# Small TensorE products dealt one head at a time among the steps of full strips

## The reference, cut to what matters

```python
q = l2norm(q) * (dk ** -0.5)          # per head, over 128 channels
k = l2norm(k)
g = jnp.cumsum(chunk(g), axis=-1)     # per head and chunk, one number per token
k_beta = k * beta[..., None]          # beta: one number per head and token
cq = rmsnorm(c_q, mla_q_norm_g)       # latent rows, 3 x 128 channels
ckv = rmsnorm(c_kv, mla_kv_norm_g)    # 2 x 128 channels
o_a = rmsnorm(o_a, gdn_norm_g) * silu(gate_a)     # per head
```

## Time and profile before

| | |
|---|---|
| median of three executions | 3966.07 us (3965.75 to 3969.32) |
| the profiled execution | 3973.19 us, span 3971.4 us |
| mean granted TensorE clock | 0.978 |
| TensorE busy | 3838.2 us of the span |
| VectorE, ScalarE busy | 2845.7 us, 1585.9 us |

### The profile page before, as it was taken

The page is one execution under the profiler, slowest core; times in us unless marked ns, Lnnn a source line. Parts: engine busy times, 40 slices in busy tenths (PEclk is TensorE's granted clock), DMA queues, the critical chain, the costliest instruction groups (busy, mean ns, idle before and its releaser), DMA issues.

```text
span 3971.4 us, 61257 instructions
## 1 busy us (share of the span) xinstructions
PE 3838.2 (97%) x21282; PEld 3185.6 (80%) x21282; DVE 2845.7 (72%) x5169; ACT 1585.9 (40%) x2439; POOL 88.2 (2%) x101
## 2 busy tenths in 40 slices
PE   8999999899989999999999999999979999999998
PEld 7897789545887888888888888888748888888887
DVE  6442266895788789999887777777463997777776
ACT  5201053231219444444484444444321094444443
POOL 0000000000000000000000000000400000000000
PEclk9899999999999999999999999999979999999999
DMA  5214455475433666666625656666764516666664
GB/s 193 80 45 131 154 182 159 139 239 184 144 113 127 191 197 195 191 190 192 193 77 176 189 188 188 189 190 191 176 237 158 167 58 194 188 188 190 189 187 152
DMA packets 203773, 666.53 MB, mean 168 GB/s; under 512 B 35920, under 2 KB 46176, under 8 KB 202480
## 3 DMA queue, kind: packets, MB, share of 16 engines
q1 hardware_dynamic: 166816, 602.71, 48.2%
q0 software_dynamic: 12496, 52.53, 4.3%
q10 hardware_dynamic: 24320, 9.37, 0.9%
HBM read 637.34 MB, written 26.15 MB: 167 GB/s over the span
## 4 chain that ended last, share of the span: by engine, by line
PE 88%; DVE 9%; ACT 1%; DMA 1%; issue 1%; DVEq 0%; SPq 0%; ACTq 0%; POOLq 0%
PE psum L1083 27%; PE psum L1069 17%; PE psum L1071 9%; PE psum L641 7%; PE psum L720 4%; PE psum L695 4%; PE psum L1160 4%; PE psum L1251 3%; PE psum L1149 2%; DVE arena L2351 1%; PE psum L1049 1%; DVE arena L2352 1%; PE psum L1128 1%; DVE arena L2353 1%; PE psum L1425 1%; PE psum L750 1%
## 5 line engine op out<-in xcount | busy, mean ns | idle before, releaser
L1083 PE MATMUL psum<-rows_split_odd,coef_split 128*128 128x512 f32 x2400 | 590.6, 396 | 3.6 <-DVE rows_split_odd L2495 3.6
L1083 PE MATMUL psum<-rows_split,coef_split 128*128 128x512 f32 x2208 | 532.1, 390 | 0.3 <-issue 0.3
L2500 DVE TENSOR_REDUCE work<-psum 128x256 f32<-128x512 f32 x360 | 249.1, 692 | 394.1 <-PE psum L1071 393.0
L1083 PEld LDWEIGHTS psum<-rows_split_odd,coef_split 128*128 128x128 f32 x2400 | 437.8, 188 | 105.0 <-issue 6.8
L1069 PE MATMUL psum<-input_split,rows_split 128*128 128x512 f32 x1440 | 513.9, 397 | 1.2 <-DVE rows_split L2495 1.2
L1069 PE MATMUL psum<-input_split,rows_split_odd 128*128 128x512 f32 x1440 | 510.0, 393 | 0.0
L1710 ACT ACTIVATE work<-work 128x256 f32<-128x256 f32 x360 | 151.1, 420 | 875.8 <-DVE work L2500 875.8
L2495 DVE TENSOR_TENSOR rows_split_odd<-ring,rows_split_odd 128x1024 fp32r<-128x1024 f32 x380 | 462.6, 1218 | 8.9 <-ACT rows_split_odd L1512 8.9
L1083 PEld LDWEIGHTS psum<-rows_split,coef_split 128*128 128x128 f32 x2208 | 402.0, 188 | 81.4 <-issue 0.9
L1512 ACT ACTIVATE rows_split_odd<-ring 128x1024 fp32r<-128x1024 f32 x380 | 401.3, 1057 | 155.8 <-PE psum L1083 155.4
L2495 DVE TENSOR_TENSOR rows_split<-ring,rows_split 128x1024 fp32r<-128x1024 f32 x364 | 443.0, 1217 | 5.4 <-ACT rows_split L1512 5.4
(11 more groups left out here) (446 smaller groups left out, 5295.0 us busy)
## 6 DMA issues: line engine op xcount, KB each, us to landing
ring<-in_u SPq DMA_DIRECT2D x384, 512.0 KB, 3.6
ring<-in_v SPq DMA_DIRECT2D x384, 512.0 KB, 3.5
ring<-in_w SPq DMA_DIRECT2D x372, 512.0 KB, 3.6
scratch_inj<-stage ACTq DMA_DIRECT2D x16, 512.0 KB, 5.3
arena<-scratch_inj POOLq DMA_DIRECT2D x7, 1024.0 KB, 7.7
scratch_cm<-work POOLq DMA_DIRECT2D x8, 512.0 KB, 5.4
scratch_cm<-arena POOLq DMA_DIRECT2D x8, 512.0 KB, 5.2
arena<-scratch_parked POOLq DMA_DIRECT2D x4, 1024.0 KB, 7.8
```

The lines of the kernel that those rows point to most:

```text
L1083: last = mm(bank(2 + 2 * i + f), CFR[:, b, c, P * i:P * i + P], parts[:, v, 512 * f:512 * f + 512], start=(first and c == 0 and v == 0), s ...
L2500: dve.tensor_reduce(AC[:, b, :], bank(b).rearrange("p (x t) -> p t x", x=2), AX, ALU.add)\
```

## The change

Inside `spread` and `row_sums` a step of a strip is issued behind every second small product, so four steps per call, and the counts of the `fill` calls behind are lowered to match. The exps have one step of `gates` behind every pair. The mark of the last small product stays on that product. At the injection the modulation generator is made earlier, behind `turn_groups(7)`, with its waits, and four row products are issued ahead of each of the injections 5, 6 and 7; 36 steps instead of 48 are left for the time of the scan.

```diff
--- before.py
+++ after.py
@@ -732,17 +732,21 @@
 
             sel = col1("sel", NH, P, parts=8)
 
-            def spread(off, rows, n, s):
+            def spread(off, rows, n, s, work):
                 for h in range(NH):
                     last = mm(PS(off + n * h, n), sel[:, h, :], rows, start=(n * h % 512 == 0), stop=True,
                               skip_group_check=True)
-                L.mark(last, s)
-
-            def row_sums(out, src, first):
+                    if h == NH - 1:
+                        L.mark(last, s)
+                    fill(work, h % 2)
+
+            def row_sums(out, src, first, s, work):
                 for h in range(NH):
                     last = mm(out, pick[:, 7 - h:15 - h], src[:, h, :], start=(first and h == 0), stop=(h == NH - 1),
                               skip_group_check=True)
-                return last
+                    if s and h == NH - 1:
+                        L.mark(last, s)
+                    fill(work, h % 2)
 
             def row_part(b, w, k, f):
 
@@ -775,38 +779,39 @@
 
             evacuated()
             L.take("head_squares")
-            row_sums(bank(2)[0:8, 0:S], SQ[:, 0:8, :], True)
+            misc = strip(8, 8, H)
+            row_sums(bank(2)[0:8, 0:S], SQ[:, 0:8, :], True, None, misc)
             L.take("head_squares")
-            L.mark(row_sums(bank(2)[0:8, S:2 * S], SQ[:, 8:16, :], False), "head_sums")
-            misc = strip(8, 8, H)
-            fill(misc, 24)
+            row_sums(bank(2)[0:8, S:2 * S], SQ[:, 8:16, :], False, "head_sums", misc)
+            fill(misc, 16)
             L.take("head_rstd")
-            spread(1024, HV[:, 0, :], S, "heads_spread")
-            fill(misc, 8)
+            spread(1024, HV[:, 0, :], S, "heads_spread", misc)
+            fill(misc, 4)
             L.take("heads_scaled")
-            spread(1024, HV[:, 1, :], S, "heads_spread")
-            fill(misc, 16)
+            spread(1024, HV[:, 1, :], S, "heads_spread", misc)
+            fill(misc, 12)
             L.take("heads_scaled")
             L.take("beta_row")
-            spread(1024, ROWS[:, 0, :], S, "rows_spread")
-            fill(misc, 8)
+            spread(1024, ROWS[:, 0, :], S, "rows_spread", misc)
+            fill(misc, 4)
             L.take("beta_evacuated")
             L.take("decay_rows")
-            spread(1024, ROWS[:, 1, :], S, "rows_spread")
-            fill(misc, 8)
+            spread(1024, ROWS[:, 1, :], S, "rows_spread", misc)
+            fill(misc, 4)
             rowsum(SQM, 3, S)
             L.take("row_exps")
             L.take("decay_evacuated")
+            gates = strip(8, 8, H)
             for h in range(NH):
                 mm(PS(1024 + P * h, P), sel[:, h, :], ROWS[:, 2, P:S], start=(h % 4 == 0), stop=True,
                    skip_group_check=True)
                 mm(PS(2048 + P * h, P), sel[:, h, :], ROWS[:, 3, 0:P], start=(h % 4 == 0), stop=True,
                    skip_group_check=True)
+                fill(gates, 1)
             for c in range(2):
                 last = pe.transpose(PS(3072 + 8 * c, 8), ROWS[:, 1, P * c:P * c + P], ident[0:8, 0:8])
             L.mark(last, "exps_spread")
-            gates = strip(8, 8, H)
-            fill(gates, 16)
+            fill(gates, 8)
             rowsum(SQM, 2, S)
             fill(gates, 24)
             L.take("exps_evacuated")
@@ -903,12 +908,12 @@
             rows = first_rows()
             fill(rows, 4)
             L.take("squares")
-            L.mark(row_sums(bank(2)[0:8, 0:S], SQO, True), "rowsum")
             uq = strip(8, 3, CQ)
+            row_sums(bank(2)[0:8, 0:S], SQO, True, "rowsum", uq)
             fill(uq, 24)
             L.take("head_rstd")
-            spread(1024, HVO, S, "heads_spread")
             uq = strip(8, 3, CQ)
+            spread(1024, HVO, S, "heads_spread", uq)
             fill(uq, 24)
             kn = strip(8, 2, CKV)
             fill(kn, 16)
@@ -1462,13 +1467,15 @@
             turn_groups(6)
             inject(4)
             turn_groups(7)
+            rows = modulation()
+            pe.wait_ge(sem("modulation_operands"), 5)
+            pe.wait_ge(sem("tokens_evacuated"), 8)
             for q in range(5, 8):
+                fill(rows, 4)
                 inject(q)
             pe.wait_ge(sem("injected_evacuated"), 8)
             pe.wait_ge(sem("injected_back_evacuated"), 8)
-            pe.wait_ge(sem("modulation_operands"), 5)
-            rows = modulation()
-            fill(rows, 48)
+            fill(rows, 36)
             L.take("scanned")
             pe.wait_ge(sem("toep_loaded"), 16 * 32)
             for e in range(2):
```

## The result

| | before | after |
|---|---|---|
| median, same chip | 3966.88 us (3965.75 to 3969.32) | 4013.53 us (4011.65 to 4014.72) |
| ratio, 95% interval | | 1.0109 (1.0097 to 1.0121) |
| the profiled execution | 3973.19 us | 4011.65 us, span 4009.9 |

The change costs 46.6 us by the medians and 38.5 us between the two profiled executions. The difference of 8 us lies in the executions that were profiled: that of before was 6.3 us over its median, that of after 1.9 us under. The ratio with its interval stands for 38 to 48 us. Forecast were 3969.0 us and a range up to 3981, so the result is far outside.

The account below looks back on a forecast made before the run. TensorE, busy 97% of the span, was taken to bound the kernel. Terms -5.3 + 4.3 + 2.9 - 3 = -1 us for the profiled execution; charging 4 us against the median gave +3 us, 3969 us, range 3954 to 3981.

Parts of the forecast that it names:

- Where I choose: Norm stage spreads: whether the mix holds the clock; took half the gain, 4 us, with the stretch 5.0 instead of 3.7 us.
- The clock term: Norm stage: three low stretches between 113.94 and 156.52 lose 8.5 us at half speed; half the gain, 4 us, was taken.
- The waits: Norm stage: fewer covering steps; head sums 0.7 us, first spread 0.3, decay row 0.1 more than now, latent sums 0.4 more.
- Latent row sum: Two-step row sum at 172.3: a new wait of 3.9 us, followed by low clock costing 1.7 us.
- Output norm: Near 350 us: small strips' third step 1.2 us later, TensorE idle 4.0 us, low clock behind it 1.7; sum +2.9 us.
- Injection: Near 2880 us: row products bring the clock back, but not at once; -3 us, between -5.2 and +5.1.
- 8-column sums: Norm stage head sums: eight columns did not hold the clock down, so strips among them buy nothing a row shows.
- Profile against median: Whole kernel: profiled execution is 7.1 us over the median, whose runs likely have fewer falls; 4 us charged.
- A: Norm stage and injection: clock holds as meant, median runs have the profiled falls; 3958.5 us, chance 0.22.
- B: Latent sums and output norm: waits of 3.9 and 4.0 us decide; +11.2 us, 3977 us, chance 0.23.
- C: Whole kernel: TensorE's idle time alone sets its clock, so falls stay and waits add; 3975.5 us, chance 0.05.
- D: Head sums: the change does not do what it says; 8-column products need no strips, that half empty; no chance given.

Follow-up runs that it names:

- after_64_rows: Changed kernel with all its dealing, but spreads and exps read 64 rows (8 of values, 56 of zeros): 3987.11 us, ratio 1.0037.
- after_full_rows: Changed kernel with all its dealing, but spreads and exps read 128 rows, one memset added: 3977.03 us, ratio 1.0013.
- coarse: Changed kernel with two strip steps behind the fourth and eighth small product instead of one behind every second: 3985.36 us, ratio 1.0041.
- inj_undone: Changed kernel with the injection as before, no row products ahead of injections 5 to 7: 4009.00 us, ratio 1.0095.
- sums_alone: Kernel before with strip steps dealt among the 8-column row sums only: 3974.25 us, ratio 1.0006.
- full_rows: Kernel before, undealt, but spreads and exps read all 128 rows, zeros behind the eighth, one memset added: 3962.98 us, ratio 0.9983.

## Why the prediction was wrong

**What failed is one step, "Where I choose", with the price under it.** The prediction took a spread at 0.46 us a product and a step at 0.44, as the earlier trace rows has them in rows of their own kind, and let the mixture last "5.0 instead of 3.7 us", which is 5.4 us with the fourth step. With that step it lasts four times 1.68, 6.7 us, at 1.00, and 10.1 us in the first spread (116.64 to 126.8), where the clock fell inside. No term existed for a change of shape. In after there are 16 pairs in the norm stage's spreads and 9 in the exps and the transposes behind them, where before had 4 and 1: 20 new ones at 0.39 us. Among the head sums there are 8 in place of 1, and in the output norm's row sums, which end just before the 371.74 us read above, 4 in place of 1: 10 new ones at 0.29 (1.59 us for two sums and a step, against about 1.30). Together 10.7 us. The Trainium skill, "TensorEngine Tiling (Array Packing)", section "Key Properties", says that changing the tiling mode drains TensorE. Its section "Available Configurations" lists arrays of 64 and of 32 rows as modes beside those of 128. The trace agrees if products over 8 or 64 rows count as such modes: 0.33 us of idle weight load at each change, and no difference between 8 and 64 rows. That a mode is what changes here, no run shows by itself. The prediction did not weigh this page.

**The clock term had the wrong sign.** Expected were 4.3 us back of 8.5. What came is 64.8 us at 0.50 in place of 27.3: (64.8 - 27.3) / 2 = 18.8 us lost, an estimate that is up to 0.8 us too high, since 1.52 us of the 64.8 are a wait. The upper bound of the prediction charged a mixture at 0.50 with 1.3 us in each of four spreads, 5.2 us in all, and did not ask whether the longer mixture would lengthen the low stretches. after_64_rows and after_full_rows show that the cause is the 8-row product: with 64 or 128 rows, dealt in the same way, the spreads hold 1.00. coarse shows that with 8 rows the fineness of the dealing matters as well (30.7 us at 0.50, not 64.8). Why, and how much of the 18.8 us it brings, is not settled.

The sum of the norm stage: 10.7 + 18.8 + 0.6 + 0.6 + 1.5 for the waits = 32.2 us, where 31.8 were lost. So close a fit is partly luck, since the clock term is rough to about a microsecond.

**The waits were right, apart from what low clock covered.** Head sums 0.7 us predicted, 0.62 measured. First spread 0.3: none in after, where the clock stretched the cover, 0.22 in after_full_rows. Decay row 1.6: 1.52. Latent row sum 3.9: 1.55 in after, 3.89 in after_full_rows, and in that kernel 3.4 us at 0.50 follow it from 167.3 us, as the prediction charged. In after itself 1.00 follows this wait from 198.1 us, so that sign did not show. All this was small beside what was missing. Two readings of before were off without changing the sum. The fall at 147.00 lies inside the fourth spread (144.31 to 148.83), not behind it. And of the 9.4 us of gate steps ahead of the latent row sum, only the 4.5 us up to 167.47 are at 0.50.

**Output norm**: +2.9 us predicted, +2.5 measured, but made up otherwise. The wait ahead of the third step is 2.51 us, not 4.0 (the 0.52 us behind it stand in before as well), and 13.7 us at 0.50 lie around it:

```profile
393.98 10.69 PE L720 MATMUL psum<-arena,ring 128*128 128x256 f32 x36 [2.51 <-DVE arena L2203]
405.18 5.02 PE L720 MATMUL psum<-arena,ring 128*128 128x256 f32 x22 [0.52 <-DVE arena L2203]
```

The low clock goes on costing behind that step: the next wait ends at 405.18 us where before has 368.23, 37.0 us later. By injection 3 these further 2.6 us are gone again; where, no row here shows.

**Injection**: -3 us was taken between bounds of -5.2 and +5.1. The upper bound came true, +5.9 us by the trace: three groups of row products, 1.87 us later each, all at 0.50. inj_undone gives 4.5 by the medians.

**8-column sums**: "putting strips among them buys nothing that a row shows" held. In sums_alone's profile it costs 2.8 us up to the first spread and 6.4 us up to the output norm's row sums. The run's time is 4.5 us longer by the medians, which its interval does not tell from no change.

**Profile against median**: the prediction feared that executions at the median have fewer falls to win back and charged 4 us. The gap was 8 us. The later runs of before fit that reading: the fastest took 3965.09 us at a mean granted clock of 0.979, the slowest 3980.01 us at 0.976.

**The rivals.** A (3958.5) is excluded. B (3977) had the right sign by the wrong place: its waits are a few microseconds. C (3975.5) said that TensorE's idle time alone sets its clock. The Trainium skill's "TensorE: Matmul & The Clock Gate", section "The HAM clock gate (the "warmup" mystery)", has the gate follow how busy the engine has been. Read as busy time, the trace contradicts it: 10.20 us busy of 10.20 at 0.50 from 119.50. And full_rows lifts the clock with the very same count of products. D is out: strips among 8-row products do change the clock, in the other direction. The four chances add up to 1.00 and left nothing for a loss above B's, which is what came.

## What to carry to other kernels

Small products of one shape belong together: dealt singly among full ones, each product that breaks the shape pays about 0.2 us on the way in and again on the way out, and a mixture with 8-row products can also keep the clock low. Where a contraction has few rows, padding it with zeros to 128 costs no TensorE time in this kernel (3.62 against 3.72 us) and took away both the changes and the falls of the norm stage's spreads and exps; try it before any reordering. And a cost read from a group of like instructions is not the cost of the same instruction between unlike ones.

## What was not expected of the hardware

- A change between a product of 8 or 64 rows and one of 128 holds back the next weight load: 0.33 us idle, 0.39 us per pair at 1.00. With 8 columns in place of 8 rows it is 0.29 us per pair.
- TensorE busy all the time stood at 0.50 for 10.2 us (from 119.50) where float32 products of 8 rows were dealt among full ones. The same order with 64 or 128 rows ran at 1.00.
- The costs are not linear in how finely work is dealt: half the changes in the spreads and sums gave back 28 of 46.6 us.
- Three of four ring slots' worth of row products could be had ahead of injection 4; the next one cost 7.82 us.
